# Experts two at a time in column halves of TensorE, in plain fp32, with overflow weights gathered: a two-block model on one core

## The reference

```python
g_w, g_idx = lax.top_k(g_prob, 1)                 # one of 4 groups
e_w, e_idx = lax.top_k(jax.nn.softmax(e_sel), 2)  # two of its 8 experts
expert = (g_idx * 8 + e_idx).reshape(-1)          # 512 (token, expert) pairs
hg = lax.ragged_dot(xs, w_gate, sizes)            # per expert (n, 1024) x (1024, 256)
hu = lax.ragged_dot(xs, w_up, sizes)              #            (n, 1024) x (1024, 256)
ys = lax.ragged_dot(jax.nn.silu(hg) * hu, w_down, sizes)   # (n, 256) x (256, 1024)
```

## Time and profile before

| what | value |
|---|---|
| time, median of 3 runs | 1314.3 us (1313.84 to 1318.7) |
| time of the profiled execution | 1313.62 us |
| its span | 1311.8 us |
| PE, DVE, ACT, POOL busy, share of the span | 94%, 71%, 58%, 11% |
| first and last matmul of the experts' blocks | 971.95 us, 1288.72 us |
| DMA rate from 1000 to 1200 us | 366 GB/s |

### The profile page before, as it was taken

The page is one execution under the profiler, slowest core; times in us unless marked ns, Lnnn a source line. Parts: engine busy times, 40 slices in busy tenths (PEclk is TensorE's granted clock), DMA queues, the critical chain, the costliest instruction groups (busy, mean ns, idle before and its releaser), DMA issues.

```text
span 1311.8 us, 22319 instructions
## 1 busy us (share of the span) xinstructions
PE 1233.8 (94%) x8926; PEld 1137.7 (87%) x8926; DVE 929.0 (71%) x1386; ACT 754.6 (58%) x1085; POOL 143.9 (11%) x157
## 2 busy tenths in 40 slices
PE   6999989999999999899999979998879999999993
PEld 4888889999998888889999978897768999999992
DVE  4564577887546554578987465655569999999994
ACT  5443545656434444446555445445448888888883
POOL 5000000000000000000300000000001233223220
PEclk9999999999998999899999989999789999999997
DMA  9443456776553443368665544422218999999982
GB/s 278 161 170 120 157 165 174 220 210 193 175 177 107 161 161 103 124 191 237 193 183 177 178 128 129 129 66 97 97 64 304 370 364 373 370 366 350 361 319 96
DMA packets 199521, 262.21 MB, mean 200 GB/s; under 512 B 18655, under 2 KB 177931, under 8 KB 185979
## 3 DMA queue, kind: packets, MB, share of 16 engines
q1 hardware_dynamic: 186608, 232.99, 54.1%
q0 software_dynamic: 12448, 27.66, 6.0%
q10 hardware_dynamic: 363, 0.14, 0.0%
HBM read 257.61 MB, written 19.40 MB: 211 GB/s over the span
## 4 chain that ended last, share of the span: by engine, by line
PE 78%; DVE 9%; ACT 5%; issue 4%; DMA 2%; DVEq 0%; SPq 0%; POOLq 0%; ACTq 0%
PE ps L728 20%; PE ps L729 19%; PE ps L730 19%; ACT whi L700 3%; DVE wlo L709 2%; PE ps L2441 2%; PE ps L2443 2%; PE ps L2442 2%; PE ps L670 2%; DMA raw<-in_w_exp_up 2%; PE ps L2001 2%; PE ps L2002 1%; PE ps L2068 1%; PE ps L2393 1%; PE ps L2039 1%
## 5 line engine op out<-in xcount | busy, mean ns | idle before, releaser
L709 DVE TENSOR_TENSOR wlo<-raw,whi 128x2048 fp32r<-128x2048 f32 (+1 forms) x186 | 421.7, 2269 | 177.8 <-ACT whi L700 177.6
L700 ACT ACTIVATE whi<-raw 128x2048 fp32r<-128x2048 f32 (+1 forms) x186 | 352.1, 1894 | 182.5 <-PE ps L730 176.4
L728 PE MATMUL ps<-xhi,whi 128*128 128x272 f32 (+2 forms) x1424 | 429.0, 301 | 20.3 <-DVE xlo L724 10.9
L729 PE MATMUL ps<-xlo,whi 128*128 128x272 f32 (+2 forms) x1424 | 412.9, 290 | 0.0
L730 PE MATMUL ps<-xhi,wlo 128*128 128x272 f32 (+2 forms) x1424 | 411.3, 289 | 0.0
L728 PEld LDWEIGHTS ps<-xhi,whi 128*128 128x128 f32 x1424 | 274.3, 193 | 34.8 <-issue 25.1
L729 PEld LDWEIGHTS ps<-xlo,whi 128*128 128x128 f32 x1424 | 274.1, 192 | 0.9 <-issue 0.5
L730 PEld LDWEIGHTS ps<-xhi,wlo 128*128 128x128 f32 x1424 | 273.6, 192 | 0.0
L728 PE MATMUL ps<-whi,xs_hi 128*128 128x256 f32 x560 | 161.4, 288 | 2.7 <-DVE xs_lo L1899 2.7
L730 PE MATMUL ps<-whi,xs_lo 128*128 128x256 f32 x560 | 158.5, 283 | 0.0
L729 PE MATMUL ps<-wlo,xs_hi 128*128 128x256 f32 x560 | 158.3, 283 | 0.0
(11 more groups left out here) (410 smaller groups left out, 1821.6 us busy)
## 6 DMA issues: line engine op xcount, KB each, us to landing
raw<-in_w_up SPq DMA_DIRECT2D x88, 512.0 KB, 5.1
raw<-in_w_exp_gate SPq DMA_DIRECT2D x35, 1024.0 KB, 5.8
raw<-in_w_exp_up SPq DMA_DIRECT2D x35, 1024.0 KB, 5.1
raw<-in_w_exp_down SPq DMA_DIRECT2D x35, 1024.0 KB, 6.2
raw<-in_w_in SPq DMA_DIRECT2D x33, 1024.0 KB, 5.4
ada<-in_w_ada POOLq DMA_DIRECT2D x48, 512.0 KB, 5.0
raw<-in_w_down SPq DMA_DIRECT2D x16, 896.0 KB, 4.6
raw<-in_w_out SPq DMA_DIRECT2D x8, 1024.0 KB, 5.0
```

The costliest lines, as they stand in the source:

```text
L700: act.activation(whi[SLOT[n]][:, 0:nk, :], raw[n % RAW][:, 0:nk, :], ACT.Copy).then_inc(s_w_hi.sem, s_w_hi.event(CHUNKS[n]))
L709: dve.tensor_tensor(wlo[SLOT[n]][:, 0:nk, :], raw[n % RAW][:, 0:nk, :], whi[SLOT[n]][:, 0:nk, :].bitcast(F32), ALU.subtract).then_inc(s_w_ ...
L728: pe.matmul(dst, ah, bh, start=first, stop=False, **kw)
L729: pe.matmul(dst, ah, bl, start=False, stop=False, **kw)
```

## The change

The experts' part is rewritten; nothing ahead of the sorting changes but two weight splits that leave it.

- Weights are no longer split. PE multiplies the loaded chunk as it is, as plain fp32, which the machine runs as two passes per matmul (the trace has two records for each).
- Two experts form a pair. The first one's tokens (64 at most) are the stationary operand of columns 0 to 63 of the array, the second one's that of columns 64 to 127; their results lie in the two partition halves of one PSUM bank. Matmuls of the two alternate.
- There are 16 pairs of experts and 4 pairs of overflow halves (each for tokens 65 to 128, 129 to 192 or 193 to 256 of an expert), put in at positions 5, 9, 13 and 17: 20 pairs. Each has 6 chunks: gate, gate, up, up, down, down.
- Chunks go through a ring of 10 buffers: the 4 of `raw`, 2 of `wx` (where the third split copy was) and 4 where `whi` and `wlo` were. Chunk n may be loaded when PE has used chunk n-10.
- The 24 overflow chunks keep their places in the ring, but POOL loads them by gather: an indirect DMA with one row number for each of 128 partitions. Where no overflow is there, all row numbers lie past the bound, so nothing is fetched. POOL issues the 6 gathers of pair p+2 ahead of the scatter of pair p; PE waits for all six before that pair's gate product.
- `turn(p-1)` moves into the middle of `widen("ga", p)`, and `narrow(p-1)` ahead of `widen("gb", p)`. One scatter serves a pair, so there are 20 and not 35.
- The sorted tokens are one tensor `Xs`; the four sorting products of a step add up in one PSUM bank, and eight banks are used.

Six gathers, each with a wait for a buffer, stand between the scatters of the third and the fourth pair. The diff, cut to its core:

```diff
-OVER = 3
-NBLK = NEXP + OVER
+CAP = 64
+OVER = 8
+NPAIR = (NEXP + OVER) // 2
+WBUF = 10
...
+def pair_list():
+
+    out = [(2 * i, 2 * i + 1) for i in range(NEXP // 2)]
+    for q, at in enumerate((5, 9, 13, 17)):
+        out.insert(at, (NEXP + 2 * q, NEXP + 2 * q + 1))
...
 
-CHUNKS = chunk_list()
+PAIRS = pair_list()
+DEST_AT = [a // 2 for a, _ in PAIRS]
+CHUNKS = [(g, j) for g in GROUPS for j in range(3 if g[0] == "down" else 1)]
+EXPERTS_AT = len(CHUNKS)
+CHUNKS += [((kind, 0, e), 0) for ab in PAIRS for kind in ("ga", "gb", "dn") for e in ab]
...
+
+        flat = lambda t: t[:, :, :].rearrange("p a b -> p (a b)")
+        one_, two_ = SLOT[EXPERTS_AT - 2], SLOT[EXPERTS_AT - 1]
+        ebuf = [flat(raw[(EXPERTS_AT + u) % RAW]) for u in range(RAW)] + [flat(t) for t in wx] + \
+               [flat(t) for s_ in (one_, two_) for t in (over_whi[s_], over_wlo[s_])]
+        ebuf_sem = [s_raw[(EXPERTS_AT + u) % RAW] for u in range(RAW)] + s_wx + [s_x, s_prm]
...
+
+        def buffer_free(eng, n):
+
+            u = (n - EXPERTS_AT) % WBUF
+            if n - WBUF >= EXPERTS_AT:
+                eng.wait_ge(s_w_used.sem, s_w_used.after(CHUNKS[n - WBUF]))
+            elif u < RAW:
+                eng.wait_ge(s_w_lo.sem, s_w_lo.after(CHUNKS[n - RAW]))
+            elif u < RAW + 2:
+                eng.wait_ge(s_hg_o.sem, s_hg_o.after(1))
+            else:
+                eng.wait_ge(s_w_used.sem, s_w_used.after(CHUNKS[EXPERTS_AT - (2 if u < RAW + 4 else 1)]))
...
+            for n in range(EXPERTS_AT, len(CHUNKS)):
+                if on_pool(n):
+                    continue
+                buffer_free(sp, n)
+                kind, _, e = CHUNKS[n][0]
+                u = (n - EXPERTS_AT) % WBUF
+                sp.dma_start(ebuf[u], expert_rows(kind)[P * e:P * e + P, :]).then_inc(ebuf_sem[u], 16)
...
+
+            def load_overflow(p):
+
+                if PAIRS[p][0] == NEXP:
+                    pool.wait_ge(s_over.sem, s_over.after())
+                for n in range(EXPERTS_AT + 6 * p, EXPERTS_AT + 6 * p + 6):
+                    kind, _, e = CHUNKS[n][0]
+                    buffer_free(pool, n)
+                    pool.indirect_dma_start(out=ebuf[(n - EXPERTS_AT) % WBUF], out_offset=None, in_=expert_rows(kind),
+                                            in_offset=bass.IndirectOffsetOnAxis(ap=wrow[:, e - NEXP:e - NEXP + 1], axis=0),
+                                            bounds_check=NEXP * P - 1, oob_is_err=False).then_inc(s_small, 16)
+
+            for p in range(NPAIR):
+                if p + 2 < NPAIR and PAIRS[p + 2][0] >= NEXP:
+                    load_overflow(p + 2)
+                if p == 0:
+                    pool.wait_ge(s_dest.sem, s_dest.after(0))
+                if PAIRS[p][0] == NEXP:
+                    pool.wait_ge(s_dest.sem, s_dest.after(1))
+                pool.wait_ge(s_y_left.sem, s_y_left.after(p))
+                pool.wait_ge(s_y_right.sem, s_y_right.after(p))
+                d = DEST_AT[p]
+                pool.indirect_dma_start(out=spread[:, :], out_offset=bass.IndirectOffsetOnAxis(ap=dest[:, d:d + 1], axis=0),
+                                        in_=Yb[:, p % 2, :], in_offset=None, bounds_check=SLOTS - 1,
+                                        oob_is_err=False).then_inc(s_scat[p % 2], 16)
 
 
...
+            for p in range(NPAIR + 1):
+                if p >= 1:
+                    act.wait_ge(s_hut.sem, s_hut.after(p - 1))
+                    if p >= 3:
+                        act.wait_ge(s_w_used.sem, s_w_used.after(("dn", 0, PAIRS[p - 3][1]), 0))
+                    act.activation(hut[:, (p - 1) % 2, :, :].rearrange("p j n -> p (j n)"), ps[2 + (p - 1) % 2][:, 0:256], ACT.Copy).then_inc(s_hut_copied.sem, s_hut_copied.event(p - 1))
+                    act.wait_ge(s_w_used.sem, s_w_used.after(("dn", 0, PAIRS[p - 1][1]), 0))
+                    if p >= 3:
+                        act.wait_ge(s_scat[(p - 1) % 2], 16 * ((p - 1) // 2))
+                    act.activation(Yb[:, (p - 1) % 2, 0:512], ps[4 + 2 * ((p - 1) % 2)][:, :], ACT.Copy).then_inc(s_y_left.sem, s_y_left.event(p - 1))
+                if p < NPAIR:
+                    act.wait_ge(s_w_used.sem, s_w_used.after(("gb", 0, PAIRS[p][1]), 0))
+                    if p >= 2:
+                        act.wait_ge(s_hu.sem, s_hu.after(p - 2))
+                    act.activation(sg[:, p % 2, :], ps[p % 2][:, 0:256], ACT.Silu).then_inc(s_silu.sem, s_silu.event(p))
+                if p + 2 < NPAIR:
+                    take_a(p + 2)
             act.preload_act_table_set("natural_log_exp_and_others")
             for t in range(2):
...
+                dve.tensor_scalar(wrow_f[:, :], found[:, :, 0], float(P), tok4[:, 0, 0:1], ALU.mult, ALU.add)
+                r(dve.tensor_scalar(wskip[:, :], found[:, :, 0], 0.0, 1.0e6, ALU.is_equal, ALU.mult))
+                dve.scalar_tensor_tensor(wrow[:, :], wrow_f[:, :], -129.0, wskip[:, :], ALU.add, ALU.add).then_inc(s_over.sem, s_over.event())
...
+                ns = [CHUNK_NO[((kind, 0, e), 0)] for e in PAIRS[p]]
+                for n in ns:
+                    expert_landed(pe, n)
+                cs = slice(0, 256) if kind == "ga" else slice(256, 512)
                 for j in range(8):
+                    for half_, n in enumerate(ns):
+                        mm = pe.matmul(ps[p % 2][CAP * half_:CAP * half_ + CAP, cs], xsl[:, p % 2, half_, j, :],
+                                       ebuf[(n - EXPERTS_AT) % WBUF][:, 256 * j:256 * j + 256], start=(j == 0), stop=(j == 7))
+                        if j == 7:
+                            mm.then_inc(s_w_used.sem, s_w_used.event(CHUNKS[n]))
+                    if between is not None and j == 3:
+                        between()
...
+                for h in range(2):
+                    for j in range(2):
+                        for half_, n in enumerate(ns):
+                            rows = slice(CAP * half_, CAP * half_ + CAP)
+                            mm = pe.matmul(ps[4 + 2 * (p % 2) + h][rows, :], hut[:, p % 2, j, rows],
+                                           ebuf[(n - EXPERTS_AT) % WBUF][:, 1024 * j + 512 * h:1024 * j + 512 * h + 512],
+                                           start=(j == 0), stop=(j == 1))
+                            if h == 1 and j == 1:
+                                mm.then_inc(s_w_used.sem, s_w_used.event(CHUNKS[n]))
...
+            for p in range(NPAIR + 1):
+                if p < NPAIR:
+                    widen("ga", p, (lambda: turn(p - 1)) if p else None)
+                else:
+                    turn(p - 1)
...
+                if p >= 1:
+                    narrow(p - 1)
+                if p < NPAIR:
+                    widen("gb", p)
```

More of the change, by code:

```diff
@@ L120, with on_pool @@
 PAIR, PREV = bank_pairs()
[L123 to L132, removed]
-    return out
-CHUNKS = chunk_list()
+def pair_list():
+    out = [(2 * i, 2 * i + 1) for i in range(NEXP // 2)]
+    for q, at in enumerate((5, 9, 13, 17)):
+        out.insert(at, (NEXP + 2 * q, NEXP + 2 * q + 1))
+    return out
+PAIRS = pair_list()
[3 more added lines that the diff above has]
+CHUNKS += [((kind, 0, e), 0) for ab in PAIRS for kind in ("ga", "gb", "dn") for e in ab]
 CHUNK_NO = {c: n for n, c in enumerate(CHUNKS)}
[L139 to L142, removed]
+SLOT = [n % SPLIT for n in range(EXPERTS_AT)]
+def on_pool(n):
+    return n >= EXPERTS_AT and CHUNKS[n][0][2] >= NEXP
 class Signal:
@@ L197, in build @@
         m = [ada_at, ada_at + 2 * 8 * CW * 4]
-        whi.append(sb("whi_x", [P, 8, CW], F32R, at=m))
-        wlo.append(sb("wlo_x", [P, 8, CW], F32R, at=m))
+        wx = [sb(f"wx{i}", [P, 8, CW], at=m) for i in range(2)]
         XT = sb("XT", [P, KT, T])
@@ L330, in build @@
         s_ada = [sem(f"s_ada{i}") for i in range(ADA)]
+        s_wx = [sem(f"s_wx{i}") for i in range(4)]
         s_x = sem("s_x")
@@ L2446, in _, with widen @@
-            for b in range(NBLK + 1):
-                if b < NBLK:
-                    widen("ga", b)
-                if b == 0:
+                        o = pe.matmul(ps[SORT_BANK[k]][:, :], src[:, t, k::KT], place[:, t, :], start=(u + t == 0), stop=(u + t == 2))
+                o.then_inc(s_sorted.sem, s_sorted.event(k))
+            def widen(kind, p, between=None):
+                if kind == "ga":
+                    pe.wait_ge(s_slot_a.sem, s_slot_a.after(p))
+                    pe.wait_ge(s_slot_b.sem, s_slot_b.after(p))
+                    if p >= 2:
+                        pe.wait_ge(s_hu.sem, s_hu.after(p - 2))
+                ns = [CHUNK_NO[((kind, 0, e), 0)] for e in PAIRS[p]]
+                for n in ns:
+                    expert_landed(pe, n)
+                cs = slice(0, 256) if kind == "ga" else slice(256, 512)
+                for j in range(8):
+                    for half_, n in enumerate(ns):
[5 more added lines that the diff above has]
+                        between()
@@ new lines, in turn, with narrow @@
```

(19 more changed lines are left out.)

317 lines of the change are left out of this document (119 added, 198 removed).

## The result

The changed kernel took 1310.3 us in the median against 1316.9 for the kernel before (18 runs each; the changed kernel's lie from 1306.3 to 1315.7, but for one of 3794 that the comparison leaves out). The ratio is 0.9945, interval 0.9926 to 0.9964: faster by 0.55%, where I had forecast 1.7%. The sign and the range were right, two thirds of the gain are missing.

What follows compares the result with a forecast made beforehand. PE's matmuls set the pace before, with transfers close; after the change, transfers. 1252 us without stalls, plus 33 for overflow pairs (1285.5) and 4.5 for the clock: span 1290.0, plus 1.8 outside it: 1292 us; range 1264 to 1322.

Steps and rivals of the forecast that it cites:

- PE per pair: Experts' stage: matmuls alternating between column halves run side by side, 10.9 us per pair; 21.4 if they don't.
- Rival 1: Experts' matmuls: halves don't overlap or the clock stays low, 21.4 us per pair, time 1432 us; chance 0.14.
- rival 5: Overflow gathers fetch in spite of the bound: 24 chunks more, 69 us more transfer, about 1325; chance 0.02.
- Transfers per pair: Experts' weight loads: six chunks of 2.87 us at 366 GB/s, 17.2 us per pair, so DMA sets the pace.
- what would make it wrong: Load queue: the deeper ring carries well over 373 GB/s; 0.1 us per chunk is 8 us over 82 chunks.
- The four overflow pairs: Late gathers and ring places with nothing to fetch idle the load queue 8.3 us per overflow pair, 33 us for four.
- B: The pair directly ahead of an overflow pair; its gate landing starts the count, its down product ends 22.7 us later.
- A: The pair two ahead of an overflow pair; its down product ends at 7.4 us and releases the last gathers.
- landing: Overflow gathers: they land 4 us after POOL is done, from a span of 1.1 to 4.9.
- O: The overflow pair itself; its gate waits for gathers until 15.3 us into the count and is done at 19.2.
- The clock: Experts' stage: a burst starting at low clock loses about 2 us; half counted as low, 4.5 us in all.
- rival 4: Experts' stage: every burst starts at the low clock, 2 us more wherever half were counted, 1305 us; chance 0.12.

## Why the forecast was wrong

**PE per pair: right.** 3.4 to 3.6 us per product, 10.9 us per pair. Rival 1 is out. So is rival 5: the software queue carried 27.67 MB, against 27.66 in the kernel before.

**Transfers per pair: mis-sized, in the kernel's favour.** "At the 366 GB/s of a long stretch [...] a chunk is 2.87 us." It is 2.51; 82 chunks give 29 us back. A rate measured while the engine set the pace is a lower bound, not the queue's. The DMA share seemed to say otherwise, but it hardly tells the two apart: 0.98 at 366 GB/s and 1.01 at 418. The prediction had named this as what would make it wrong.

**The four overflow pairs: the step that failed.** The order of events was as predicted, its terms were too small. From t = 1025.28, gate of B landed:

| step | forecast | measured | more |
|---|---|---|---|
| gate of B with the turn | 3.9 | 5.4 (to 1030.69) | 1.5, mostly low clock |
| down of A | 3.5 | 3.6 | 0.1 |
| four gathers on POOL | 3.9 | 5.7 (to 1039.97) | 1.8 |
| landing | 4.0 | 6.2 (to 1046.13) | 2.2 |
| gate of O with the turn | 3.9 | 6.8 (to 1052.89) | 2.9, mostly low clock |
| down of B | 3.5 | 3.6 | 0.1 |

8.5 us more until the queue goes on. I had 7.8 to 8.3 us idle, it was 17.6. The landing was lost in a subtraction. The prediction has "7.4 in a full one, so 1.1 to 4.9 after POOL is done": the 4.9 takes off the 2.54 us of a scatter beside a split, while the gathers were priced at 0.97. With that it is 6.4 after POOL, and 6.2 was measured. The reason given, "The fetches of B are still under way then", does not hold either: from 1033.5 to 1038 us the DMA share is 0.12. What the gathers meet are the two chunks behind B's, which SP sends as soon as up of B is done. POOL's step has two more parts: a gather starts 1.30 us after the one before and not 0.97 (1.0 us over four), and the first starts 0.8 us after down of A ends. **The clock** was booked apart as 4.5 us in all, for half of the bursts; the two bursts that feed the chain lose 4.0 us at each pair (5.4 and 6.8 against 4.1), so rival 4 was the better case, and its bursts lie just where nothing covers them. Its price does not follow from the text, though: twice the 4.5 us would give 1296, not 1305. A faster queue also empties earlier, and so turns a part of its gain into idle time.

**The balance.** Forecast 318.6 us from first expert matmul to end. Rate -29; holes 70 instead of 33 and 4.5, +33. The end is +5 by an estimate: the forecast had 5.5 us from the last chunk's landing to the last product's end, and here the loads are through at about 1274 and the product ends at 1284.1. The last gate product falls into

```profile
1265.00:1270.00 5.00, 5.00 (x22) 2.61 (x23) 0.00 (x0) 0.38 (x1) 0.00 (x0) 0.50 1.02 424
```

and the last pair's products, not its last chunk, set the end. That makes 327.6 of the 333.1; 5.5 us are not assigned. Two errors of about 30 us with opposite signs leave the time near the forecast, so that it lies inside the stated range is luck. The tests bear out the large terms: 70 us go with the overflow pairs in all, some 40 with the wait, 20 with the landing and what hangs on it, roughly 7 with the clock. These overlap and do not add.

**What I did not question** is the wait itself. I took it as given that gate of an overflow pair waits for all six gathers, and priced it. But its own two are issued at 1021 and 1022 us and read at 1038 at the earliest; the four that make it wait are for up and down. Giving each product its own wait is worth some 40 us.

## What to carry to other kernels

Once transfers set the pace, count each place of the ring that has nothing to fetch, and ask of each wait whether the instruction reads what it waits for: here three semaphores in place of one are worth some 40 us, and two more places in the ring about as much. Read a rate as the queue's own only from a stretch in which consumers waited for it. Price a small transfer by its landing beside the loads that will run there, and a pause by its length and the slow burst behind it.

## What the runs showed of the hardware

- An indirect gather in which every row is out of bounds moves next to no bytes: the 24 of them add 3456 packets and 0.01 MB to the software queue (13744 packets, 10288 in the kernel with the gathers gone). It still needs 1.0 us of POOL, 1.3 from one to the next, and 2.1 (quiet) to 8.4 us (beside loads) to land.
- fp32 matmuls of 128 rows in the two column halves run fully side by side when they alternate: 0.215 us per pass of 256 columns for both halves, 15.5 against 10.9 us per pair without and with alternation. Written half by half they overlap only over a few records at each change of half, also between different products and banks.
- After 8.4 us of pause the clock was 0.50 for 4 us and 0.68 over the next 3. After a pause of 3.6 us the first product was slow too (5.7 us instead of 4.1).
- The loads of this one core ran at 418 GB/s over 180 us. The Trainium skill ("DMA: Bandwidth & Descriptors", Specifications) states about 358 per core, which it works out as half of a stack's 716 for two cores. Only one core runs here, where the measurement decides; no run shows what a second busy core would leave.
